# Expert weights in whole-row pieces: one pass per expert, six slots in place of twelve half pieces

## What is computed

```
def expert_choice_moe(h, w_router, w_gate, w_up, w_down):
    cap = max(1, EC_CAPACITY_FACTOR * L // N_EXPERTS)      # 64 of 512 sample rows, 16 of 128 prompt rows
    aff = softmax(h @ w_router); gate, idx = top_k(aff^T, cap)
    xs = h[idx]                                            # (expert, cap, 1024)
    hid = silu(xs @ w_gate) * (xs @ w_up)                  # 1024 -> 2816
    out = (hid @ w_down) * gate                            # 2816 -> 1024
    return zeros.at[idx].add(out)
```

## Time and profile before

| what | value |
|---|---|
| median of 3 runs | 1985.57 us (1985.0 to 1986.83) |
| profiled execution | 1986.42 us, of which the span in the profile is 1984.6 us |
| TensorE busy | 1910.4 us (96% of the span), 28594 matmul records |
| VectorE, ScalarE, GpSimd busy | 1207.5, 395.4, 394.6 us |
| DMA | 647.58 MB; from about 590 us on the 16 engines are busy nine tenths of each slice or more, at 405 to 420 GB/s |
| chain that ended last | TensorE 76%, DMA 12%, VectorE 4%, SyncE's queue 3% |
| granted TensorE clock | 0.989 of 2.4 GHz over the span, 1.00 from 650 us to 1900 us |

### The profile page before, as it was taken

How to read it: one execution, slowest core, us unless ns; L and a number is a source line. 1 busy time by engine, 2 the same in 40 slices (tenths; PEclk the granted TensorE clock), 3 DMA queues, 4 the chain that set the end, 5 groups by cost and what they waited for, 6 DMA issues and landing times.

```text
span 1984.6 us, 64364 instructions
## 1 busy us (share of the span) xinstructions
PE 1910.4 (96%) x28594; PEld 1604.4 (81%) x28594; DVE 1207.5 (61%) x1969; ACT 395.4 (20%) x909; POOL 394.6 (20%) x406
## 2 busy tenths in 40 slices
PE   8999999999997999999999999999999999999996
PEld 5888899999873888788877778779777687877874
DVE  3532441232556777687676867767677676867764
ACT  4331333122320111111111211112111111211113
POOL 3032019000411130311303113030211303112012
PEclk9999999999998999999999999999999999999998
DMA  8244542312359999999999999999999999999997
GB/s 334 86 161 151 176 129 64 107 51 79 127 220 363 412 407 419 408 411 415 408 418 409 414 412 411 415 407 420 407 411 416 407 419 408 412 414 412 414 411 288
DMA packets 150463, 647.58 MB, mean 326 GB/s; under 512 B 11420, under 2 KB 56344, under 8 KB 134024
## 3 DMA queue, kind: packets, MB, share of 16 engines
q1 hardware_dynamic: 134576, 617.71, 77.5%
q0 software_dynamic: 15648, 29.02, 5.0%
q10 hardware_dynamic: 184, 0.06, 0.0%
HBM read 632.47 MB, written 14.40 MB: 326 GB/s over the span
## 4 chain that ended last, share of the span: by engine, by line
PE 76%; DMA 12%; DVE 4%; SPq 3%; issue 3%; ACT 1%; POOL 0%; POOLq 0%; DVEq 0%; ACTq 0%
PE bank L2386 17%; PE bank L2414 16%; PE bank L1985 16%; PE bank L2403 9%; DMA ring<-in_w_exp_gate_dram 9%; PE bank L2396 6%; PE bank L2106 3%; PE bank L2252 2%; SPq L568 2%; DMA ring<-in_w_exp_down_dram 1%; PE bank L2311 1%; SPq L575 1%; PE bank L1956 1%; PE bank L1967 1%; DMA x_in<-in_x_sample_dram 1%
## 5 line engine op out<-in xcount | busy, mean ns | idle before, releaser
L1715 DVE TENSOR_TENSOR sums<-ring 128x704 f32<-128x704 f32 x744 | 608.5, 886 | 191.8 <-PE bank L2403 168.2
L2386 PE MATMUL bank<-ring,hid_t 128*32 128x256 f32 x8184 | 480.4, 379 | 12.9 <-DVE hid_t L1787 7.2
L2414 PE MATMUL bank<-ring,xs_t 128*32 128x352 f32 x5952 | 453.1, 459 | 0.0
L2386 PEld LDWEIGHTS bank<-ring,hid_t 128*32 128x32 f32 x8184 | 380.6, 110 | 79.4 <-issue 9.8
L2414 PEld LDWEIGHTS bank<-ring,xs_t 128*32 128x32 f32 x5952 | 307.5, 110 | 128.3 <-issue 7.6
L2403 PE MATMUL bank<-sums,xu_a 128*32 128x176 f32 x5952 | 296.5, 313 | 18.3 <-issue 17.8
L2403 PEld LDWEIGHTS bank<-sums,xu_a 128*32 128x32 f32 x5952 | 241.9, 110 | 42.6 <-issue 40.3
L791 POOL TENSOR_TENSOR small<-kpow 128x2 f32<-128x2 f32 x31 | 10.4, 334 | 993.1 <-DVE out_rows L1846 868.1
L1167 ACT ACTIVATE v_both<-bank 128x176 f32<-128x176 f32 x31 | 9.9, 318 | 856.0 <-PE bank L2403 856.0
L2396 PE MATMUL bank<-ring,xu_a 128*32 128x176 f32 x1984 | 173.8, 313 | 0.0
L1985 PE MATMUL bank<-act_hi,wt_hi 128*128 128x320 f32 x448 | 138.8, 310 | 0.8 <-DVE rtmp L1526 0.8
(11 more groups left out here) (366 smaller groups left out, 2398.5 us busy)
## 6 DMA issues: line engine op xcount, KB each, us to landing
ring<-in_w_exp_gate_dram SPq DMA_DIRECT2D x128, 1408.0 KB
ring<-in_w_exp_up_dram SPq DMA_DIRECT2D x128, 1408.0 KB
ring<-in_w_exp_down_dram SPq DMA_DIRECT2D x96, 1536.0 KB
ring<-in_w_exp_down_dram SPq DMA_DIRECT2D x32, 1024.0 KB
raw_t<-in_w_ada_dram SPq DMA_DIRECT2D x16, 1024.0 KB, 5.3
raw_t<-in_w_in_dram SPq DMA_DIRECT2D x14, 1024.0 KB, 5.2
a_raw<-in_w_ada_dram SPq DMA_DIRECT2D x8, 1024.0 KB, 16.5
raw_t<-in_w_branch_gate_dram SPq DMA_DIRECT2D x8, 1024.0 KB, 5.4
```

The lines of the kernel that those rows point to most:

```text
L1715: nc.vector.tensor_tensor(sums[:, (N_SUM * i + j) % SUM_SLOTS], w[:, k, :, n, :], w[:, kk, :, nn, :], ALU.add if sign > 0 else ALU.subtrac ...
L2386: ins = mm(bank[5 + x // 2][c * Q:(c + 1) * Q, x % 2 * DC:(x % 2 + 1) * DC], hid_t[:, f, x * Q:(x + 1) * Q], w[:, j, c * DC:(c + 1) * DC], ...
L2414: ins = mm(bank[UP_BANK[x]][c * Q:(c + 1) * Q, 0:FC], xs_t[:, x, k * Q:(k + 1) * Q], w[:, kk, c * FC:(c + 1) * FC], start=k == 0, stop=k = ...
```

## The change

A step becomes a whole expert, so that the loops of all engines run 15 times with twelve pieces of twice the size. A gate or up piece is two whole rows of 2816 values per partition, 22528 bytes in one run; a down piece is 6 or 5 rows, 24576 or 20480 bytes. There are six slots. The loop's order is g0 d0 g1 d1 g2 d2 g3 d3 u0..u3. Every unit product of the gate is 352 columns wide instead of 176, and as eight banks don't hold ten of them side by side with the rest, six sum units are cut over banks (`PLACES`), down to 64 columns. The ring `sums` has four slots of double size, and the wait for a free one is now per sum (`sum_used`). `combine` works on copies that ScalarE makes with 14 evictions in place of 6. Expert 0's gate and up products are both done as plain products with eight pieces; the fifth (`u0`) lands in the area of `sums`, asked for once the residual rows are written (`s_acc`), and no request waits for the gathered sample rows any more. The core of the diff:

```diff
-RING = 12
-STEPS = 2 * NE
-FIRST = 8
+RING, STEP_N, FIRST = 6, 12, 8
+SPARE_AT = 4
-DOWN_AT, DOWN_N = (0, 3, 6, 9), (3, 3, 3, 2)
+DOWN_AT, DOWN_N = (0, 6, 11, 16), (6, 5, 5, 6)
-STEP = (("g", 0), ("d", 0), ("g", 1), ("d", 1), ("g", 2), ("d", 2), ("d", 3), ("g", 3), ("u", 0), ("u", 1), ("u", 2), ("u", 3))
+STEP = (("g", 0), ("d", 0), ("g", 1), ("d", 1), ("g", 2), ("d", 2), ("g", 3), ("d", 3), ("u", 0), ("u", 1), ("u", 2), ("u", 3))
-N_SUM, SUM_SLOTS = 6, 8
+N_SUM, SUM_SLOTS = 6, 4
+UNITS = (R11, R22, V2, V1, R21, V4, V3, V5, V6, R12)
+PLACES = {R11: ((3, 0, 0, 352),), R22: ((4, 0, 0, 352),), R21: ((7, 0, 0, 352),), R12: ((0, 0, 0, 352),),
+          V5: ((1, 0, 0, 352),), V6: ((1, 0, 0, 352),),
+          V2: ((2, 0, 0, 192), (3, 352, 192, 160)), V1: ((2, 192, 0, 192), (4, 352, 192, 160)),
+          V4: ((2, 384, 0, 128), (0, 352, 128, 160), (7, 352, 288, 64)), V3: ((6, 256, 0, 256), (7, 416, 256, 96))}
...
+            sp.wait_ge(e_used, 1)
+            gate_up(ring[0], "g", 0, 0, 0, e_landed[0])
+            sp.wait_ge(e_used, 2)
+            gate_up(ring[2], "g", 2, 0, 0, e_landed[2])
+            sp.wait_ge(e_used, 4)
+            gate_up(ring[1], "g", 1, 0, 0, e_landed[1])
+            gate_up(ring[3], "g", 3, 0, 0, e_landed[3])
+            sp.wait_ge(e_used, RING)
+            for lt in range(NT):
+                sp.wait_ge(s_h2w[lt], 16)
+            gate_up(ring[4], "u", 1, 0, 0, e_landed[4])
+            sp.wait_ge(s_acc, 16 * NT)
+            gate_up(extra, "u", 0, 0, 0, e_extra)
+            gate_up(ring[5], "u", 2, 0, 0, e_landed[5])
+            sp.wait_ge(e_used, RING + 1)
+            gate_up(ring[0], "u", 3, 0, 0, e_landed[0])
...
                 for j in range(first, last):
+                    q = N_SUM * i + j
+                    if q >= SUM_SLOTS or not isinstance(r, int):
+                        dve.wait_ge(sum_used, 4 * N_SUM * r + q - SUM_SLOTS + 1)
...
+            def iteration(r, ahead):
+
+                if ahead:
+                    nc.vector.tensor_copy(idx_gather[:].unsqueeze(1), idx_all[:, 2:NE, :][:, expert_at(r), :]).then_inc(e_idx, 1)
+                for i in range(1, KT // 2):
+                    piece_sums(r, i, 0, N_SUM)
+                dve.wait_ge(e_used, STEP_N * r + RING + FIRST + POS["g", 3] + 1)
+                combine(r)
+                rows(r)
+                if ahead:
+                    rows_ahead(r + 2)
+                    piece_sums(r + 1, 0, 0, SUM_SLOTS)
+                hidden_samples(r)
+                if ahead:
+                    piece_sums(r + 1, 0, SUM_SLOTS, N_SUM)
+                hidden_prompt(r)
...
             def up(r, i, slot):
...
                     if i == 0:
+                        if x < 2:
+                            pe.wait_ge(e_evict, EVICT * r + (4, 10)[x])
+                        else:
+                            pe.wait_ge(e_out, NX * r + NX)
...
-            with pe.Fori(0, STEPS - 1) as r:
-                for t in range(RING):
-                    slot = (FIRST + t) % RING
+            with pe.Fori(0, NE - 1) as r:
+                for t in range(STEP_N):
+                    slot = slot_of(t)
```

More of the change, by code:

```diff
@@ new lines, in _ @@
+            sp.wait_ge(s_acc, 16 * NT)
[3 more added lines that the diff above has]
+            gate_up(ring[0], "u", 3, 0, 0, e_landed[0])
+            for t in range(3):
+                piece(RING + 2 + t, t, 0, 0)
+            with sp.Fori(0, NE - 2) as e:
+                for t in range(3, STEP_N):
+                    piece(STEP_N * e + FIRST + t + 1, t, e, 0)
+                for t in range(3):
+                    piece(STEP_N * e + STEP_N + FIRST + t + 1, t, e, 1)
@@ L601, in _ @@
+            for t in range(3, STEP_N):
+                piece(STEP_N * (NE - 2) + FIRST + t + 1, t, NE - 2, 0)
+            for i in range(5):
+                sp.wait_ge(e_used, STEP_N * (NE - 1) + FIRST + i + 1)
+                down(slot_of(i), LAST_AT[i], LAST_N[i], NE - 1, 0)
             for j, lt in enumerate(Y_ORDER):
@@ new lines, in _ @@
+            nc.vector.memset(unit(V5)[:, :, Q // 2:], 0.0)
+            nc.vector.memset(unit(V6)[:, :, 0:Q // 2], 0.0)
+            rows_ahead(1)
+            dve.wait_ge(e_used, RING + SPARE_AT + 1)
+            piece_sums(0, 0, 0, SUM_SLOTS)
+            dve.wait_ge(e_used, RING + FIRST)
+            for x in range(NX):
+                dve.wait_ge(e_silu if x < 2 else e_comb, x % 2 + 1)
+                product(x, UP0_AT[x], e_mul if x < 2 else s_up2)
+            for x in range(NX):
+                dve.wait_ge(e_mul if x < 2 else s_up2, x % 2 + 1)
+                hidden_transpose(x)
@@ L1879, in _ @@
[L1879 to L1894 removed]
+            tick(nc.vector.tensor_copy(gate_cur[:], gate_all[:, NE - 1, :]))
@@ L1922, in _ @@
             dve.wait_ge(s_fg, 16 * 5)
-            dve.wait_ge(e_gath, 16 * NI * (NE - 1) + 32 + 16 * NX)
-            for x in range(NX):
-                dve.wait_ge(e_out, done + x + 1)
-                nc.vector.tensor_tensor(out_rows[:, x, :], out_rows[:, x, :], x_g[:, x, :], ALU.add).then_inc(e_rows, 1)
-            dve.wait_ge(e_hid, NX * STEPS)
             for j in range(NT):
@@ L2398, in gate @@
-                for j in range(N_SUM):
-                    b, o = SUM_AT[j]
-                    if j % 2 == 0:
-                        pe.wait_ge(sums_done, 4 * N_SUM * r + N_SUM * i + j + 2)
-                    for c in range(4):
-                        ins = mm(bank[b][c * Q:(c + 1) * Q, o:o + FN], unit(j)[:, i, :], sums[:, (N_SUM * i + j) % SUM_SLOTS, c, :],
-                                 start=i == 0 and j % 2 == 0, stop=i == KT // 2 - 1, skip_group_check=True)
-                ins.then_inc(e_used, 1)
```

576 lines of the change are left out of this document (277 added, 299 removed).

## The result

| | before | after |
|---|---|---|
| median | 1986.2 us (4 runs) | 2128.1 us (2126.8 to 2130.1, 4 runs) |
| ratio | | 1.071, 95% interval 1.069 to 1.073 |
| profiled execution, span | 1986.42, 1984.6 us | 2126.82, 2125.0 us |
| branch at the end of TensorE's loop, first to last | 682.7 to 1951.3 us, 31 passes | 772.7 to 2080.1 us, 15 passes |

A forecast was written before the change was run, and what follows sets the result against it. TensorE and DMA were taken as limits side by side, TensorE binding after the change. Start 667.8 + 5.5, loop 1262.4, gathers and jumps 63, end 43.9 gave a 2042.6 us span, 2043 median; range 1985 to 2080.

The forecast's parts named there:

- The side: Whole kernel: slower with chance 0.8, faster 0.15, same 0.05.
- likeliest case: Whole kernel: TensorE bound at 88.4 us per expert, 2043 us, own range 2015 to 2080; chance 0.6.
- Jumps of the loop: TensorE's jump back: the doubled body is fetched anew, about 2.5 us each, 14 times, 35 us; bounds 0 and 6.9 each.
- Start: Ahead of the loop: expert 0's whole sample product, loop begins at 667.8 us, first-pass g0 waits 5.5 more.
- Gathers: TensorE's trickle in g1 beside GpSimd's six gathers: 2.0 us per expert, bounds 0 and 3.3, 14 times: 28.
- Waits of TensorE on sums: V6 in each of four gate pieces: sum 0.6 us late, 2.4 us per expert; bounds 0 and 1.5 per piece.
- Wait of u0 for the rows: u0's third tile waits for the scaled rows to leave the banks: 0.8 us per expert, at most 3.
- Bigger packets: Weight DMA: 13.2 ns per packet, so 3.1 us less per expert, pace 82.3 us; no term in the sum.
- rival 3: Loop: TensorE's waits hidden, gathers free, DMA pace of 82.3 us decides: 1952 us; stops under 3.4 us; chance 0.15.
- What bounds the kernel now: Loop before the change: TensorE (80.76 us per expert plus 3.5 trickle) and DMA (85.40) are limits side by side.
- Rival 2: TensorE's jumps: code kept or its fetch hidden, no 35 us, 2008 us, gathers' bounds 1985 to 2026; chance 0.2.

The follow-up runs named there:

- unrolled: The changed kernel with TensorE's loop written out 15 times, so that no jump is left: 2031.0 us.
- before_two_steps: The kernel before with only TensorE's loop changed, two steps per pass (2 x 1580 instructions): 2073.8 us, ratio 1.045.
- hold_back: The changed kernel with the requests for u0, u2 and what follows held until the first sample rows are gathered: 2120.9 us, ratio to before 1.068.
- order_r22: The changed kernel with TensorE's loop written out, requests held until the first sample rows are gathered, unit R22 moved behind V2: 1989.7 us, ratio to before 1.0017.
- light_after: order_r22 with half of the up product in TensorE's loop left out, all weights still read: 1984.8 us, ratio 0.999.
- before_light: The kernel before with half of the up product in the loop left out: 1989.8 us, ratio 1.002.
- gathers_later: order_r22 with the list for the six gathers copied ahead of g3's sums, so GpSimd gathers two pieces later: 1991.0 us.
- order_not_held: order_r22 without the hold, so u0 and u2 are asked for ahead of the first sample rows: 2013.7 us, ratio 1.013.
- looped_order_hint: order_r22 with the changed kernel's loop in place of the written-out one, and a prefetch hint for the jump back: 2051.4 us, ratio 1.032.
- hint: The changed kernel with TensorE told at the top of each pass where its loop jumps back to: 2080.8 us.

## Why the prediction was wrong

- **The side, and the likeliest case.** Slower was right, and so was its mechanism: TensorE bound, the DMA no longer. 2128 us lies outside 1985 to 2080.
- **"Jumps of the loop"** is the step that failed, as the term that was mis-sized. That the new body has to be fetched at each jump was right, and so were the two packets. "It is about 2.5, and 14 x 2.5 = 35": by unrolled it is 97 us, 6.9 each. Two things were short. The branch takes 6.0 us, and the idle stretch is 5.1, inside my bounds (0 to 6.9) but near the high end. My working had 1.0 us for each packet and the rest for weight packets ahead of it; by before_two_steps, where those are a third as long and the branch as long as here, that isn't what the rest is, so a sum that came out at 5.1 would have done so by luck. And behind a stop of 5 us the clock was at 0.50, for which I had no term: 6.9 - 5.1 = 1.8 us more. The range then cut the jumps at 5 us each, below the bound that the text itself had.
- **"Start"**: "plus 2 for the first rows' gather, which now runs beside a piece". It took 12 and 13.5 us in place of 3. I had taken the gather as one small transfer beside a piece; it is a row of small packets, with other small transfers ahead of it on its queue, and each passes a weight packet of 0.8 us. hold_back, which has 3.1 us again, shows that the early requests are the cause.
- **"Gathers"**: 2.9 for 2.0 us, where the kernel before has 3.3 to 3.5, so wider units gain little. The rows had the number; the discount was a guess.
- **"Waits of TensorE on sums" and "Wait of u0 for the rows"**: right, 0.52 for 0.6 and 0.55 for 0.8, and order_r22 shows that V6's is a wait for its slot (g2 5.94 us).
- **"Bigger packets"**: the price per packet was wrong, without weight in the sum. It was carried over from 1010 bytes to sizes where light_after and before_light differ by nothing. In rival 3 it would have made 1952 us; order_r22, which has neither the stops at the jumps nor V6's nor the trickle, ends at 1990.
- **"What bounds the kernel now"**: half right. before_light shows one limit, the weights. It would have said at once that nothing on the way of the change could win more than the few us that a request is earlier, while everything on TensorE beyond 85.4 us per expert is lost in full.
- **Two sums of the rivals don't come out.** Rival 2 without a cost of the gathers is 2008 - 28 = 1980 us, not 1985. And "88.2" is 88.4 by the likeliest case itself, which makes the room of rival 3 3.6 us and not 3.4. Neither bears on the forecast.

**What stays open.** What fills the branch beside its two packets: they take 1.9 of its 6.0 us, and the rest is not the weight packets' length. Why order_r22 and gathers_later have no trickle and order_not_held and looped_order_hint do, with the gathers at the same place in g1. In order_r22 the last two gathers take GpSimd 1.72 and 1.23 us instead of 0.84; whether a fuller DMA queue is what slows and so defuses them wasn't tried. Nor was a body of a size between 1580 and 2830.

## What to carry to other kernels

Count the instructions of a loop's body on each engine before a loop is merged: a body that stays where it is held costs nothing at its jump, one that doesn't costs its engine the whole way of a fetch, and the slow clock behind it, in every pass. Ask which limit the kernel has by taking work away from the other one; a 14 us cut that changes nothing says more than two busy shares near 1. And a small transfer that many wait for belongs ahead of the large requests: here its price was one large packet of the other queue for each small packet that it and its own queue still had.

## What the runs showed of the hardware that was not expected

- A written-out loop of 15 x 2830 instructions on TensorE ran without any stop for its code, with one instruction packet per 7.9 us (151 in 1200 us), while one jump back kept the branch for 6.0 us and TensorE idle for 4.8 to 5.4 us; a hint at the top of the pass brought that to 3.7 and to 2.1 to 3.2 us. The branch takes 6.0 us with weight packets of 0.25 us and of 0.77 us alike.
- While weights stream on one queue and small transfers on another, as many packets of the one pass as of the other (249 and 234 in 14.8 us): 3 us became 12 to 13.5 for a gather of 128 rows.
- TensorE's clock was at 0.50 for 3.4 us behind a stop of 5.3 us, and behind stops of 2.1 to 3.2 us (hint) it stayed at full speed in 5 passes of 14. In before_light and light_after, where it idles for several us in each pass, it averages 0.92 and 0.90 over the expert shown.
- Six indirect gathers of GpSimd stop TensorE and VectorE together for 2 to 3 us, in groups of a few records per 0.7 us, in most of the kernels here (not in order_r22 and gathers_later); six plain transfers of the same shape don't.
- Packets of 22528 bytes move the weights no faster than those of 5632: 85.5 and 85.3 us per expert, 412 GB/s both.
